# Hybrid decoder layer: half of the sample attention's value pages moved from TensorE to GpSimd, the other half in events of two page steps, weight ring of four loads

## The reference, cut to what matters

```python
k_past = cache_k[l][page_table].reshape(b_s, past_len, N_ATTN_HEADS, HEAD_DIM)   # 8 samples x 8 pages x 128 positions
v_past = cache_v[l][page_table].reshape(b_s, past_len, N_ATTN_HEADS, HEAD_DIM)
...
p = jax.nn.softmax(s.reshape(b, H, qc, -1), axis=-1).reshape(s.shape)
return jnp.einsum('bhqkj,bhqkjd->bhqd', p, vs.astype(f32))
```

## Time and profile before

| what | value |
|---|---|
| median of 3 runs | 1788.47 us (1785.48 to 1790.24) |
| profiled execution, span from first to last instruction | 1787.6 us |
| TensorE busy | 1762.0 us, 99% of the span |
| VectorE busy | 1194.6 us, 67% |
| ScalarE busy | 912.3 us, 51% |
| GpSimd busy | 215.6 us, 12%, nearly all before 440 us |
| TensorE clock | 0.995 of full speed over the span |
| DMA | 421.39 MB, mean 236 GB/s |

### The profile page before, as it was taken

The page is one execution under the profiler, slowest core; times in us unless marked ns, Lnnn a source line. Parts: engine busy times, 40 slices in busy tenths (PEclk is TensorE's granted clock), DMA queues, the critical chain, the costliest instruction groups (busy, mean ns, idle before and its releaser), DMA issues.

```text
span 1787.6 us, 35222 instructions
## 1 busy us (share of the span) xinstructions
PE 1762.0 (99%) x14526; PEld 1712.9 (96%) x14526; DVE 1194.6 (67%) x1679; ACT 912.3 (51%) x1724; POOL 215.6 (12%) x127
## 2 busy tenths in 40 slices
PE   8999999999999999999999999999999999999997
PEld 8999999999998989889999999999999999999997
DVE  6468998999887656744754666666666666444444
ACT  5544556555676656633454655454554554434442
POOL 2145644554000000000000000000000000000000
PEclk8999999999999999999999999999999999999999
DMA  8589987888689999696575487777777776655553
GB/s 250 171 273 330 311 277 260 279 284 272 207 251 352 291 303 323 220 308 208 174 233 166 135 282 222 236 224 223 228 233 221 222 237 196 223 177 185 163 182 98
DMA packets 398273, 421.39 MB, mean 236 GB/s; under 512 B 13041, under 2 KB 375985, under 8 KB 397073
## 3 DMA queue, kind: packets, MB, share of 16 engines
q10 hardware_dynamic: 284480, 285.62, 50.1%
q1 hardware_dynamic: 113280, 132.85, 22.9%
q0 software_dynamic: 352, 0.67, 0.2%
HBM read 400.70 MB, written 18.66 MB: 235 GB/s over the span
## 4 chain that ended last, share of the span: by engine, by line
PE 87%; DVE 8%; ACT 2%; DMA 1%; issue 1%; SPq 0%; ACTq 0%; DVEq 0%; POOL 0%; POOLq 0%
PE gemm L1770 28%; PE gemm L1771 27%; PE gemm L1772 27%; DVE w_lo L1204 3%; PE side L2027 2%; PE side L1732 1%; DVE sc_flat L1401 1%; ACT w_hi L774 1%; DVE conv_out L1196 1%; DMA kv<-in_cache_v 1%; DVE u L1196 1%; DMA xtok<-in_x_prompt 0%; DVE un L1524 0%; PE side L1923 0%; DVE y L1196 0%
## 5 line engine op out<-in xcount | busy, mean ns | idle before, releaser
L1204 DVE TENSOR_TENSOR w_lo<-raw,w_hi 128x1024 fp32r<-128x1024 f32 (+1 forms) x562 | 732.2, 1306 | 547.1 <-ACT w_hi L774 546.0
L1770 PE MATMUL gemm<-x_hi,w_hi 128*128 128x264 f32 x3312 | 953.7, 288 | 5.7 <-DVE w_lo L1204 3.7
L1771 PE MATMUL gemm<-x_lo,w_hi 128*128 128x264 f32 x3312 | 938.7, 283 | 0.0
L1772 PE MATMUL gemm<-x_hi,w_lo 128*128 128x264 f32 x3312 | 938.6, 283 | 0.0
L774 ACT ACTIVATE w_hi<-raw 128x1024 fp32r<-128x1024 f32 (+1 forms) x562 | 585.7, 1045 | 660.6 <-PE gemm L1772 659.9
L1770 PEld LDWEIGHTS gemm<-x_hi,w_hi 128*128 128x128 f32 x3312 | 624.3, 189 | 34.3 <-issue 27.5
L1771 PEld LDWEIGHTS gemm<-x_lo,w_hi 128*128 128x128 f32 x3312 | 625.1, 189 | 0.8 <-issue 0.5
L1772 PEld LDWEIGHTS gemm<-x_hi,w_lo 128*128 128x128 f32 x3312 | 621.8, 188 | 0.0
L1771 PE MATMUL gemm<-g_lo,w_hi 128*128 128x264 f32 x704 | 200.4, 285 | 0.0
L1770 PE MATMUL gemm<-g_hi,w_hi 128*128 128x264 f32 x704 | 199.9, 284 | 0.0
L1772 PE MATMUL gemm<-g_hi,w_lo 128*128 128x264 f32 x704 | 199.6, 284 | 0.0
(11 more groups left out here) (324 smaller groups left out, 1403.9 us busy)
## 6 DMA issues: line engine op xcount, KB each, us to landing
raw<-in_w_in ACTq DMA_DIRECT2D x99, 1024.0 KB, 7.0
raw<-in_w_gate ACTq DMA_DIRECT2D x44, 1024.0 KB, 5.6
raw<-in_w_up ACTq DMA_DIRECT2D x44, 1024.0 KB, 5.2
raw<-in_w_down ACTq DMA_DIRECT2D x40, 1024.0 KB, 5.5
kv<-in_cache_k SPq DMA_DIRECT2D x64, 512.0 KB, 5.6
kv<-in_cache_v SPq DMA_DIRECT2D x64, 512.0 KB, 6.0
st<-in_state_ssm SPq DMA_DIRECT2D x64, 256.0 KB, 5.6
raw<-in_w_ssm_out ACTq DMA_DIRECT2D x16, 1024.0 KB, 6.6
```

The lines of the kernel that those rows point to most:

```text
L1204: v.tensor_tensor(w_lo[:, s, 0:blk.kts, cols], raw[:, s, 0:blk.kts, cols], w_hi[:, b % RING, 0:blk.kts].bitcast(fp32), ALU.subtract).then_ ...
L1770: mm(out, w_hi[:, b % RING, k], pr.hi[:, x], start=(x == 0), stop=False)
L1771: mm(out, w_hi[:, b % RING, k], pr.lo[:, x], start=False, stop=False)
L1772: ins = mm(out, w_lo[:, s, k, cols], pr.hi[:, x], start=False, stop=(x == pr.kt - 1))
```

## The change

Samples 0 to 3 stay on TensorE, in two rounds `VE` of four events; an event holds two page steps (16 matmul instructions, no other work between them), its four pages fill all of `kv`, and they are loaded five and four blocks before the event. The 32 pages of samples 4 to 7 go to GpSimd: one load, one product of the page with its softmax weights, broadcast over the 64 numbers of a head, and, but for the first page of a sample, one addition to a running total. Two new page buffers are used in turn; pages 0 to 18 lie over the end of `gate_a` and over `m_w` (so they wait for `p_done`, and ScalarE's `ga` evacuations of tiles 8 and up wait for 19 pages), pages 19 to 31 over the sample states' buffers (they wait for `st_sum`). For each of these samples TensorE then sums the total over its 128 partitions with eight products of a 128 x 128 weight and two columns, and VectorE adds the own part. The room for the buffers comes from `raw`: LOADS is 4. The `ends` products of GpSimd stand three steps earlier in its program. The semaphore `pages_in` is merged into `vecs_in`.

```diff
-LOADS = 5
+LOADS = 4
...
+        psum_v = at("psum_v", [P, 2, AW], fp32, J1 + 7616)
+        page_g = at("page_g", [P, 2, AW], fp32, G0 + 8704)
+        page_t = at("page_t", [P, 2, AW], fp32, T0)
...
-        VG = [152 + 22 * w for w in range(4)]
+        VE = [[153, 160, 167, 174], [185, 191, 197, 203]]
+        POOLED = 19
+        PV_AT = [150 + 5 * q // 2 if q < POOLED else 203 + 11 * (q - POOLED) // 5 for q in range(4 * NPG)]
+        PV_SUM = [181, 210, 219, 235]
+        PV_CP = [1, 3, 4, 5]
+        V_ALL = 6
...
+        V_AT = [x for two in VE for x in two]
...
             def value_loads(b):
+                for v in range(8):
+                    w, k = v // 4, v % 4
+                    for half in range(2):
+                        if b != V_AT[v] - 5 + half:
+                            continue
+                        if v == 0 and half == 0:
+                            sp.wait_ge(k_red, NB * NPG)
+                        wait(sp, v_mm, v)
+                        if k == 0:
+                            wait(sp, vs_mm, w)
+                        for e in range(2):
+                            src = vc[bass.ds(page_of(2 * w + e, 2 * k + half), 1)].rearrange("g p n -> p (g n)")
+                            sp.dma_start(page_slot(2 * half + e), src).then_inc(kv_in[half], 16)
+
+            def pooled_loads(b):
+                for q in range(4 * NPG):
+                    if b != PV_AT[q]:
+                        continue
+                    if q == 0:
+                        sp.wait_ge(p_done, 1)
+                    if q == POOLED:
+                        sp.wait_ge(st_sum, 4 * NB)
+                    wait(sp, pg_add, q - 1)
+                    src = vc[bass.ds(page_of(4 + q // NPG, q % NPG), 1)].rearrange("g p n -> p (g n)")
+                    sp.dma_start(pooled_page(q), src).then_inc(kv_in[2 + q % 2], 16)
...
             def ends(b):
-                    if d == 5:
+                    if d == 2:
...
-                    if d == 6:
+                    if d == 3:
...
+            def pooled(b):
+                for q in range(4 * NPG):
+                    if b != PV_AT[q] + 2:
+                        continue
+                    j, g = q // NPG, q % NPG
+                    page, total = pooled_page(q), psum_v[:, j % 2, :]
+                    share = sc[:, g, 4 + j, :].unsqueeze(2).to_broadcast([P, HEADS, HD])
+                    if q == 0:
+                        gp.wait_ge(p_done, 1)
+                    if g == 0:
+                        wait(gp, pg_sum, j - 1)
+                    gp.wait_ge(kv_in[2 + q % 2], 256 + 16 * (q // 2 + 1))
+                    if g == 0:
+                        gp.tensor_tensor(out=by_head(total), in0=by_head(page), in1=share, op=ALU.mult)\
+                            .then_inc(pg_add, 1)
+                    else:
+                        drained(gp.tensor_tensor(out=by_head(page), in0=by_head(page), in1=share, op=ALU.mult))
+                        gp.wait_ge(pg_add, q)
+                        gp.tensor_tensor(out=total, in0=total, in1=page, op=ALU.add).then_inc(pg_add, 1)
...
                     elif pr.kind == "ga":
                         act.wait_ge(k_mul, NB * NPG)
+                        if t >= 8:
+                            act.wait_ge(pg_add, POOLED)
...
             def values(b):
-                for m in range(4 * NPG):
+                for m in range(8):
...
+                    for half in range(2):
+                        g = 2 * k + half
+                        pe.wait_ge(kv_in[half], 256 + 32 * (m + 1))
+                        for n in range(4):
+                            e, part = n % 2, n // 2
...
+                for j in range(4):
+                    if b == PV_SUM[j]:
+                        pe.wait_ge(v_cp, PV_CP[j])
+                        pe.wait_ge(pg_add, NPG * (j + 1))
+                        for t in range(AT):
+                            ins = mm(side[3][:, 2 * t:2 * t + 2], psum_v[:, j % 2, t * P:(t + 1) * P], ones[:, 0:2],
+                                     start=True, stop=True)
+                        ins.then_inc(pg_sum, 1)
```

More of the change, by code:

```diff
@@ L338, in bass_hybrid_decoder_layer @@
         K_AT = [30 + int(K_PACE * m) for m in range(NB * NPG)]
-        V_AT = [VG[w] + 2 * g for w in range(4) for g in range(NPG)]
+        V_AT = [x for two in VE for x in two]
         names = (
-            "hi_done lo_done mm_done rows_in vecs_in pages_in state_in cs_out consts_made cst_t rows_cp "
+            "hi_done lo_done mm_done rows_in vecs_in state_in cs_out consts_made cst_t rows_cp "
             "x_sum2 x_sd x_rs x_half0 x_half1 xs_pe xs_dve xs_act wrow_in raw_first x_tr h_hi h_lo cst_tr cst_cp row_tr row_cp k_out v_out q_put own_put "
@@ L485, in key_loads @@
                     if m == 0:
-                        sp.wait_ge(pages_in, 16)
+                        sp.wait_ge(vecs_in, 64)
                         sp.wait_ge(cst_tr, 2)
@@ L696, in _ @@
             gp.dma_start(pages[0:1, :], a["page_table"].rearrange("b g -> (b g)").rearrange("(o n) -> o n", o=1))\
-                .then_inc(pages_in, 16)
+                .then_inc(vecs_in, 16)
             drained(gp.affine_select(out=upper[:, :], in_=ones[:, :], compare_op=ALU.is_ge, fill=0.0, base=0,
@@ L720, in _ @@
             gp.dma_start(o["conv_sample"][0, :, 0:2, :], a["state_conv"][0, :, 1:3, :]).then_inc(cs_out, 16)
-            gp.wait_ge(vecs_in, 48)
+            gp.wait_ge(vecs_in, 64)
             for h in range(2):
@@ L769, in _ @@
                 ends(b)
+                pooled(b)
         @block.scalar
@@ L875, in time_steps @@
                 if b == DT + 2:
-                    act.wait_ge(vecs_in, 48)
+                    act.wait_ge(vecs_in, 64)
                     p = at_pair["dt", 0]
@@ L1455, in values @@
             def values(b):
-                for w in range(4):
-                    if b == VG[w] + 18:
-                        dve.wait_ge(v_mm, NPG * (w + 1))
+                for w in range(2):
+                    if b == VE[w][3] + 4:
+                        dve.wait_ge(v_mm, 4 * (w + 1))
                         own = hmask[:, :].unsqueeze(2).to_broadcast([P, 8, HD])
                         mul(by_head(kv[:, 2, 0:512]), by_head(side[3][:, :]), own).then_inc(vm_done, 1)
-                    if b == VG[w] + 21:
+                    if b == VE[w][3] + 7:
                         dve.wait_ge(vs_mm, w + 1)
@@ L1470, in values @@
                         ins.then_inc(v_cp, 1)
+                for j in range(4):
+                    if b == PV_SUM[j] + 4:
+                        dve.wait_ge(pg_sum, j + 1)
+                        n = 4 + j
+                        v.tensor_tensor(attn[:, :, TP + n], side[3][:, 0:2 * AT:2], own_t[:, n * AT:(n + 1) * AT],
+                                        ALU.add).then_inc(v_cp, 1)
             def states(b):
```

48 lines of the change are left out of this document (19 added, 29 removed).

## The result

The changed kernel takes 1798.88 us (median of 8 runs, 1793.29 to 1803.18), the kernel before 1788.17 us (8 runs): a ratio of 1.0056 with a 95% interval of 1.0042 to 1.0071. It is 10 us slower, where no change was forecast. Its profiled execution took 1797.69 us with a span of 1795.9, 8.3 us more than the span before, so the two traces can account for nearly all of it.

The account below looks back on a forecast made before the run. TensorE, 99% busy, was taken as the bound, VectorE right behind. Terms -14.7 (steps outside blocks 205 to 214) + 8.6 + 1 + 2 + 0.5 + 0.5 gave -2.1 us: 1786 us (1783 to 1793; eight in ten 1774 to 1803).

Parts of the forecast that it names:

- the norm: Blocks 205 to 214: GpSimd's instructions for pages 19 to 22 hold VectorE, making the stretch 8.6 us longer (+3.8 to +14.9).
- the ring: Weight ring of four loads: later loads are caught by ScalarE's and VectorE's lead, +0.5 us (0 to +4).
- TensorE's own work: Value steps, collapses, events and sums: 42.0 us before, 25.4 after; alone it would cut the time by 16.6 us.
- `ends` three steps earlier: Key products queue behind the end product's wait for `xdt`, and VectorE's reduction behind them: +0.5 us (0 to +3).
- Blocks 150 to 170: 17 GpSimd instructions add 14 to 25 us to VectorE, mostly hidden by its lead: +1 us (0 to +6).
- The third rival: Pages come late: when landings pass 14.5 us, events wait 1.6 us each; +11 us, 1799 us, chance 0.10.
- The change might also not do what it says: Waiting for the second step's pages may split an event into two: 2.4 us per event, +2.4 us in all.
- Full holds: Slower rival, blocks 205 to 213: each meeting costs VectorE the whole GpSimd instruction; +13 us, 1802 us, chance 0.20.
- Against: the reciprocals: Argument against whole-instruction holds in blocks 205 to 213: VectorE's five reciprocals of 1.8 us have one input.
- the +2 for a `w_lo` held in every block: Blocks 214 to 235: GpSimd back to back leaves VectorE one `w_lo` per 3.5 us; +2 us (0 to +8).
- The rivals at 1799 and 1802: Slower: late pages, 1799 us, chance 0.10; whole-instruction holds of VectorE by GpSimd, 1802 us, chance 0.20.
- the faster rival: Reciprocals and VectorE's lead cover most holds in blocks 205 to 213: -15 to -11 us, say 1776 us, chance 0.34.

Follow-up runs that it names:

- e2: The kernel before with only GpSimd's two end products moved to steps 2 and 3: 1795.74 us, ratio 1.0047 to the kernel before.
- e11: e9 with the 19 early pages kept, one page at block 203 and twelve from block 212 at 1.5 blocks each: 1790.91 us, ratio 1.0026.
- e1: The changed kernel with GpSimd's two end products put back at steps 5 and 6: 1798.99 us, ratio 1.0063 to the kernel before.
- e5: The changed kernel with every pooled product and addition cut to 16 columns, loads and waits kept: 1786.08 us, ratio 0.9988 to the kernel before.
- e14: The changed kernel with only the products and additions of pages 19 to 22 cut to 16 columns: 1790.08 us, ratio 1.0021 to the kernel before.
- e8: The kernel before with a ring of four loads and TensorE made to wait once in each of eight blocks, 320 to 460: 1814.89 us, executed once.
- e3: The kernel before with a weight ring of four loads and nothing else: 1789.57 us, ratio 1.0001 to the kernel before.
- e9: e6 with the first event's page loads issued six blocks earlier: 1792.68 us, ratio 1.0024 to the kernel before.
- e12: e11 with late pages from block 211, last sum at block 237 and VectorE's last addition two steps behind its sum: 1784.73 us, ratio 0.9981.
- e6: The changed kernel with end products at steps 5 and 6 for groups 0 to 2, 2 and 3 for groups 3 to 7: 1795.42 us, ratio 1.0032.

## Why the prediction was wrong

The forecast was 1786 us, no change; it is 1799, a loss, near the slow end of the range. In the traces the sum is +8.4 us where -2.1 was forecast. Of these 10.5 us, 5.2 are in the keys, 6.9 in blocks 150 to 205 and 0.8 in the norm; blocks 214 to 236 came out 1.9 better and the ring 0.5. By its steps:

- **TensorE's own work was right.** An event costs 1.95 us (block 185) to 2.14 (block 203), forecast 2.1; a sum 1.70 (block 219: 4.60 - 2.90), forecast 1.7.
- **The step that failed first** is "`ends` three steps earlier: ... the wait ends two steps before VectorE asks for the product: +0.5 (0 to +3)". e2 measures the move alone at 6.7 us, the change at 7.1 by block 130. I looked at when the wait ends and not at what it holds up: one reduction of VectorE, 3.2 us late, and then four key products back to back, each of which holds a VectorE that has no pause. About a third of the price, 2.5 us, is the clock.
- **The second, and the larger,** is "Blocks 150 to 170: +1 (0 to +6)", which prices VectorE alone and takes the event's pages as there. The stage lost 7.9 us beside the 7.6 that it won on TensorE. Set against the same blocks in runs without a wait: 4.0 in blocks 153 and 154, where the event's second step waits for its page and the slow products follow (4.95 and 3.02 in e11), 3.1 in blocks 170 to 173 (17.2 here; 14.1 in e1 and in e5), 0.8 in block 202 (4.15 here; 3.35 in e5). So 4.0 us are the late page; the other 3.9 go when GpSimd's instructions are short (e5), so they are holds. The third rival had the late page, but gave its loads "a lead of five blocks, 14.5 us and more" and looked for longer landings. They had no such lead: the second pair is due four blocks ahead, left 8.5 us late behind an old wait of SyncE for a state buffer, and took 10.1 us to land. And it was one event, not eight. "The change might also not do what it says, if the wait ... splits an event into two" happened, once.
- **The norm was right in size** (+9.4 for +8.6) and in its cause (9.9 us of holds for 10.5), not in its make-up, so part of the match is luck. Not seven instructions at 1.5 us held VectorE: the four additions did, with the tail of a product before two of them, 2.5 us each time. The forecast's own way without any hold gives 42.6 - 10.5 = 32.1 us; e14 measures 35.1, so the base was 3.0 us too short (1.6 of it the clock) and the holds, 8.3 us in the stage, 2.2 less than forecast. The Trainium skill (SBUF — State Buffer, Who interferes with whom) makes a hold a whole instruction. The single holds here agree: 2.1 and 2.1 us beside one addition of 2.6 and 2.7, and 3.2 and 2.5 us beside the last 1.3 and 0.6 us of a product and then an addition of 2.4. Full holds were right, and "Against: the reciprocals" too: most of the time of the four products fell on them.
- **What no step had is the clock.** By blocks: 2.5 us in block 122 (6.39 against 3.90 in block 111, which has the same side work), 1.0 in block 154 and some 0.7 in the event before it, 1.7 and 1.6 at the norm: 7.5 us together, against a net loss of 8.4. e8 shows that a wait alone makes it. The Trainium skill (TensorE: Matmul & The Clock Gate, Why this matters for your kernels) warns of idle gaps of TensorE in mid-kernel for this reason. All waits of 3.0 us or more in these traces agree, and it should have been a rival.
- The rest held: the ring +0 (e3), TensorE's own -7.1 in blocks 214 to 236 (measured -7.0; the +2 for a `w_lo` held in every block didn't come), no wait of TensorE for totals, the broadcast at no cost. ScalarE waited 2.4 us for the 19 pages.
- **The rivals at 1799 and 1802 came near the time by luck.** Neither had the end products or the clock in it. The one at 1799 is also added up short: 8 x 1.6 us and the ring's 3.5 more are 16.3, not 13, which gives 1803. And the faster rival's own terms, -14.7, -2 to +1 and +1, give -15.7 to -12.7, not -15 to -11.

Without long instructions (e5) blocks 150 to 205 are 3.2 us shorter and not 3.9, since the late page costs 4.8 us there and not 4.0. How much of the late page is the longer transfers beside the pooled pages, and how much the late issue, isn't separated; earlier loads remove the wait (e9). The stages are read from one execution of each kernel. Why a wait of about 3 us comes in some executions of the key stage and not in others, with the end products late, wasn't tried.

## What to carry over

When work is moved to an engine that shares operands with the one standing right behind the bottleneck, place it where that engine has pauses: eight instructions at the wrong blocks cost 8.3 us of their stage (e14), the pages from block 214 on nothing that shows (e12). When an instruction is moved up in an in-order queue, price what it holds up in each stage that it runs through, and the burst that follows. When steps are drawn together into one event, look up when the last load of the event really leaves, behind what already waits in its queue. And price a wait of the bottleneck TensorE by its length only while it is short: at 3.17 us and more it cost 1.6 to 2.4 us on top (e8).

## What was unexpected of the hardware

- A wait of 2.17 us left the clock as it was, one of 3.17 us halved it for most of the block behind it (e8). In between the length alone doesn't tell. The first event of the changed kernel waits 2.23 us and has slow products behind it; in e6 the same event, behind the same eight products of 32 columns of weights, waits 2.69 us, and the products behind it keep their 0.12 us:

```profile
532.25 1.07 PE L2085 MATMUL side<-kv,sc_flat 128*32 128x512 f32 x8
536.01 1.06 PE L2085 MATMUL side<-kv,sc_flat 128*32 128x512 f32 x8 [2.69 <-DMA kv<-in_cache_v]
```

The shortest wait with slow products behind it is one of 1.93 us for `w_lo` (e11). What decides between them is open.

- A pooled product (1.90 us at least) is shorter than an addition (2.41 at least) of the same 1024 columns, where I took the same for both. The additions are also the ones that grow most in the kernel, to a median of 3.25 us; that VectorE holds them is likely and wasn't tested. Their lines, each with its count and its ns min/median/max:

```profile
L812 POOL TENSOR_TENSOR psum_v<-psum_v,page_t x12: 2412/3256/3372, 729.9 to 828.1; 128x1024 f32<-128x1024 f32 x12
...
L810 POOL TENSOR_TENSOR page_t<-page_t,sc_flat x12: 1899/2070/2942, 728.0 to 825.1; 128x1024 f32<-128x1024 f32 x12
```
